# Search for the 256th value: two blocks compared on GpSimd and summed on ScalarE, totals every eleven steps of the products

## The chip, the cores and the metric

One core of one Trainium2 chip runs the whole kernel, in one launch. The metric is the device time in microseconds (us); the kernel before takes 2764.43 us, the median of 3 runs (2760.7 to 2766.13). TensorE (PE in the profile) multiplies, VectorE (DVE), ScalarE (ACT) and GpSimd (POOL) work element by element, and SyncE (SP) issues transfers. Each engine runs its own list of instructions in order, and semaphores are the only link between them: a waiting instruction holds up all that stand behind it on its engine.

## The reference

One step of a small decoder with two branches, a recurrence (RWKV-7) and sparse attention, then a feed-forward part. Two pieces matter here. First, every prompt row attends only to the 256 keys with the highest indexer score:

```python
score = jnp.einsum('bqhs,bqh->bqs', jax.nn.relu(sc), wi.astype(jnp.float32))
score = jnp.where(vis, score, -jnp.inf)
_, idx = lax.top_k(score, n_top)          # n_top = 256 for the 1040 prompt rows
```

Second, the same hidden rows (1040 prompt and 64 sample rows, 1024 wide) are multiplied by the projection `w_in`; its columns for the recurrence and the gates are what the "products" below compute, and the recurrence's columns are mixed with the row before:

```python
h = rms_norm(x, lp['norm1_g']) @ lp['w_in']
prev = jnp.concatenate([shift_prev[:, None, :].astype(p_r.dtype), p_r[:, :-1]], axis=1)
pm = p_r + (prev - p_r) * lp['rwkv_mu']
```

## The kernel before

The function `prompt_and_project` does the prompt's attention and, among it, those products. The prompt's rows lie in nine blocks of up to 128 rows, with 1040, 1024, 896, 768, 640, 512, 384, 256 and 128 visible keys. The seven blocks with more than 256 keys (`SEL`) need the 256th highest score of each row.

**The search.** `bisect` (L926) finds that score bit by bit, in 33 rounds: 1 for the sign, 31 for the bits, 1 to count what is above the result. In a round VectorE compares all scores of a row with a trial value and sums the ones (`tally`, L913; the 1040-key block has only 16 rows and is packed into 128 partitions at L914, the six others are L919). The packed block's partial sums have to be added over partitions: `total` (L520, its matmul is L522) does that on TensorE. VectorE copies the total (L923) and makes the next trial value with three tiny instructions (L938, L940, L943). A round can't begin before the one before is counted. Where each total stands among TensorE's products is written out by a counter (`tick`, L610): one every SPACING = 12 steps, a step being one of the eight 128-deep parts of a plain product.

**The products.** Meanwhile TensorE multiplies the projection. For nine pairs of weight tiles and three column blocks of 368 rows each, so 27 blocks, a block's 2 by 2 arrangement of half-size products is done with seven products in place of eight (`seven`, L468, its matmuls are L480). Product number p (0 to 6) of block m takes 1.25 us and goes to one of four PSUM banks, FA, FB, FD, FE. ScalarE takes each out of its bank (`keep`, L689, its instruction is L691). GpSimd adds the seven to four results: f16 (L857), f167 (L864), then `finish` (L820, three additions L823 to L825). ScalarE then spreads the results to their tiles (`both`, L693, through `evacuate`, L657; L678 and L680 are two of its instructions). A bank can be written again only when it was taken: product 6 needs product 2's bank, product 3 product 0's. ScalarE takes the first product of a block only after f167 of the block before (`f_mid`), and runs `both` of the block before between its products 1 and 2, so product 2 is taken only after `finish`.

GpSimd also makes the mixed weights (`weights_a`, `_b`, `_c`: L807 to L817, four additions of 128x512) for each new pair of tiles, starting in the last column block of the pair before, and the mixing with the row before for two tiles (`mix_tile`, L833 and L834), in the first column block of the next pair. The mixed tile is sent to DRAM by SyncE, and the second column block's `both` of the seventh and earlier tile pairs waits until the transfer from its buffer has landed (`pm_out`, L668). Blocks 12, 13 and 14, used below, are the last column of pair 4 and the first two of pair 5.

**After the products.** The buffer of the products is used again by the choice of the keys: `choose` (L949) may start on VectorE only when the 60th copy is done (L1031). It needs the search's result too. TensorE has six plain products (`unit`, L463) and the scores of the first attention head (L542) still to do, then waits for VectorE's first maximum (`peak_of`, L997), which stands behind three blocks of `choose`.

## Time and profile before

| what | us |
|---|---|
| time, median of 3 runs | 2764.43 |
| the profiled execution's own time | 2757.44 |
| its span, first to last instruction | 2755.6 |
| PE busy | 2571.3 (93%) |
| DVE busy | 1761.6 (64%) |
| ACT busy | 849.2 (31%) |
| POOL busy | 531.9 (19%) |
| products with the search beside them | 318.46 to 577.66 |
| from there to TensorE's next wait for VectorE's end | 577.66 to 608.95 |

The profiled execution is one run, 7.0 us below the median of the timed ones. The shares are means over a span of many stages with different limits: the change lies in a stretch of some 300 us of it.

### The profile page before, as it was taken

The page shows a single profiled execution, that of the slowest core. Times are in us where ns is not written, and L with a number is a line of the kernel's source. Part 1 is how long each engine was busy: PE and PEld are TensorE (multiplying, and loading weights), DVE is VectorE, ACT ScalarE, POOL GpSimd, SP SyncE. Part 2 cuts the span into 40 slices and gives each one's busy share as a digit, 9 for nine tenths or more (in the row PEclk, how much of TensorE's full clock was granted, in tenths as well). Part 3 has the DMA queues.
Part 4 walks back from the last instruction along what each step waited for, and adds up shares of the span by engine and source line. Part 5 has one row for each costly group of instructions (what it writes and reads, how often), then busy time and mean ns, then how long its engine had stood idle before and what let it go on. Part 6 is the DMA issues. An engine that isn't in the chain of part 4 may idle for free.

```text
span 2755.6 us, 51292 instructions
## 1 busy us (share of the span) xinstructions
PE 2571.3 (93%) x19984; PEld 1862.5 (68%) x19984; DVE 1761.6 (64%) x3313; ACT 849.2 (31%) x1914; POOL 531.9 (19%) x757
## 2 busy tenths in 40 slices
PE   8997999989997997889899999998997999999997
PEld 5553699966654323878757997565654665579997
DVE  3556888875444458676679999988732322357666
ACT  2223444325444653111112552012324421122212
POOL 0002366520000000000002662001343451011111
PEclk9998999999998986999999999999998999999999
DMA  8882012231113450000245663343355563533332
GB/s 297 308 291 79 33 64 96 66 110 37 36 52 117 162 165 16 4 27 12 96 134 181 245 241 129 122 141 119 110 170 151 190 200 108 183 130 123 123 123 71
DMA packets 95969, 348.91 MB, mean 127 GB/s; under 512 B 19560, under 2 KB 43976, under 8 KB 74032
## 3 DMA queue, kind: packets, MB, share of 16 engines
q1 hardware_dynamic: 83696, 294.50, 31.2%
q0 software_dynamic: 12032, 51.14, 5.8%
q8 instruction: 159, 2.61, 0.4%
q14 instruction: 82, 0.67, 0.1%
HBM read 289.57 MB, written 55.23 MB: 125 GB/s over the span
## 4 chain that ended last, share of the span: by engine, by line
PE 47%; DVE 7%; DVEq 3%; issue 1%; another core or an unknown queue 1%; DMA 1%; ACT 0%; POOL 0%; ACTq 0%; SPq 0%; POOLq 0%
PE banks L2553 6%; PE banks L2466 5%; PE tl_P L2553 4%; PE banks L2498 4%; PE banks L2484 3%; PE tl_P L2498 3%; PE tl_P L2466 3%; PE banks L2398 3%; PE rc_P L1580 2%; DVE arena L3092 2%; DVE tl_v L3086 2%; DVEq L3090 2%; PE tl_P L2484 2%; PE tl_P L2398 1%; PE banks L1592 1%
## 5 line engine op out<-in xcount | busy, mean ns | idle before, releaser
L162 PE MATMUL pa_PG<-pa_W,base 128*128 128x402 f32 (+1 forms) x576 | 198.5, 504 | 7.8 <-DMA pa_W<-in_w_dsa 7.7
L463 PE MATMUL dp_PS<-base,dp_W 128*128 128x368 f32 x576 | 190.0, 476 | 1.0 <-ACT dp_room_for L723 1.0
L919 DVE TENSOR_SCALAR_CACHE_REDUCE dp_EQ<-dp_SCORE,dp_trial 128x1024 f32<-128x1024 f32 (+1 forms) x186 | 176.0, 946 | 19.5 <-issue 0.5
L2466 PE MATMUL banks<-base,tl_WU 128*128 128x368 f32 x496 | 161.3, 480 | 10.1 <-issue 9.3
L162 PEld LDWEIGHTS pa_PG<-pa_W,base 128*128 128x128 f32 (+1 forms) x576 | 106.7, 187 | 94.5 <-issue 14.2
L2484 PE MATMUL banks<-base,tl_WD 128*128 128x368 f32 x484 | 154.3, 474 | 0.0
L463 PEld LDWEIGHTS dp_PS<-base,dp_W 128*128 128x128 f32 x576 | 104.7, 190 | 64.6 <-issue 8.8
L3036 POOL DMA_INDIRECT arena<-in_cache_kv,tl_PHT x128 | 121.7, 951 | 132.5 <-PE tl_P L2632 96.4
L3086 DVE MAX8 tl_v<-arena 128x8 f32<-128x4100 f32 x32 | 141.8, 4431 | 2.6 <-issue 0.7
L2466 PEld LDWEIGHTS banks<-base,tl_WU 128*128 128x128 f32 x496 | 94.9, 193 | 70.0 <-issue 14.5
L3089 DVE FIND_INDEX8 tl_i<-tl_v,arena 128x8 uint32<-128x4100 f32 x32 | 141.5, 4423 | 0.0
L3092 DVE MATCH_REPLACE8 arena<-tl_v,arena 128x4100 f32<-128x4100 f32 x32 | 141.2, 4414 | 0.0
L2484 PEld LDWEIGHTS banks<-base,tl_WD 128*128 128x128 f32 x484 | 90.5, 190 | 57.1 <-issue 3.7
L480 PE MATMUL dp_PS<-dp_room_for 128*128 128x184 f32 x648 | 111.7, 321 | 0.0
L2738 ACT ACTIVATE arena<-base 128x368 f32<-128x368 f32 x44 | 22.1, 509 | 273.4 <-DVEq L3129 143.4
L480 PEld LDWEIGHTS dp_PS<-dp_room_for 128*128 128x128 f32 x648 | 102.4, 190 | 0.0
L691 ACT ACTIVATE dp_room_for<-dp_PS 128x184 f32<-128x184 f32 x189 | 57.5, 324 | 126.5 <-PE dp_PS L480 120.7
L2705 POOL TENSOR_TENSOR base<-tl_T 128x368 f32<-128x368 f32 x36 | 30.4, 844 | 303.2 <-ACTq L2788 302.3
L2498 PE MATMUL banks<-arena 128*128 128x184 f32 x504 | 85.6, 319 | 1.4 <-DVE arena L3260 1.4
L997 DVE CUSTOM_DVE_ANT_0 dp_room_for<-dp_PS,dp_SCORE 128x1024 f32<-128x1024 f32 (+7 forms) x64 | 48.5, 758 | 57.7 <-PE dp_PS L551 50.3
L2410 PE MATMUL banks<-base,arena 128*128 128x368 f32 x256 | 81.4, 473 | 1.9 <-DMA arena<-in_wo 1.5
L2498 PEld LDWEIGHTS banks<-arena 128*128 128x128 f32 x504 | 80.0, 190 | 1.6 <-issue 1.6
(554 smaller groups left out, 5718.0 us busy)
## 6 DMA issues: line engine op xcount, KB each, us to landing
tl_WU<-in_wu SPq DMA_DIRECT2D x58, 1024.0 KB, 4.9
pa_WQ<-in_wu SPq DMA_DIRECT2D x22, 1024.0 KB, 8.3
wsum<-pa_WS SPq DMA_DIRECT2D x22, 1024.0 KB, 4.9
tl_WD<-in_wd SPq DMA_DIRECT2D x32, 704.0 KB
arena<-wsum SPq DMA_DIRECT2D x21, 1024.0 KB, 7.1
dp_W<-in_w_rw SPq DMA_DIRECT2D x15, 1024.0 KB, 6.5
arena<-in_wb SPq DMA_DIRECT2D x24, 512.0 KB, 3.8
arena<-in_wo SPq DMA_DIRECT2D x24, 512.0 KB, 3.7
```

Source lines behind the costliest of these rows:

```text
L162: last = pe.matmul(PG[0:n, c, 0:NC4], xT[:, k, r:r + n], W[:, c, k, :], start=k == 0, stop=k == KD - 1)
L463: last = pe.matmul(bank(f)[:, 0:w], W[:, t // 2 % 2, k, 128 * (t % 2):128 * (t % 2) + 128], xT[:, k, c:c + w], start=k == 0, stop=k == KD - 1)
L480: last = pe.matmul(out, weights(e, k), moving(k), start=first and k == 0, stop=k == 3, skip_group_check=True)
L919: dve.tensor_scalar(EQ[0:n, 0:m], scored_of(j), values(n, x), None, op, ALU.add, accum_out=result[0:n, x:x + 1])
L2466: last = pe.matmul(out[:, 0:W], WU[:, i % 2, o:o + 128], XN[:, k, :], start=k == 0, stop=k == KD - 1)
L2484: last = pe.matmul(out[:, 0:W], WD[:, i % 3, 128 * e:128 * e + 128], HT[:, f, :], start=f == 0, stop=f == NF - 1)
L2498: last = pe.matmul(out[:, 0:H], weights[:, k, :], moving(k), start=first and k == 0, stop=k == 3, skip_group_check=True)
L2553: last = pe.matmul(out[:, 0:H], weights[:, k, :], moving(k), start=first and k == 0, stop=k == kk - 1, skip_group_check=True)
L3036: pool.indirect_dma_start(out=KV[:, n % 16, t, :], out_offset=None, in_=I["cache_kv"], in_offset=bass.IndirectOffsetOnAxis(ap=PHT[:, 64 * ...
L3086: dve.max(v8[:, :], SC)
L3089: dve.max_index(i8[:, :], v8[:, :], SC)
L3092: dve.match_replace(SC, v8[:, :], SC, TAKEN)
```

## The change

- In each round the comparisons of the two smallest searched blocks (512 and 384 keys) leave VectorE. GpSimd writes their ones and zeros (`compare`) into a buffer that is free then, and ScalarE squares them in place with the sum as accumulator output (`count_in`).
- Three semaphores link the round: VectorE raises `trial_set` when a trial value is there, GpSimd `compared`, ScalarE `counted`, and VectorE waits for `counted` before it ends its round.
- The totals stand every 11 steps, written out ahead as `spots` (block m, product p). At a spot TensorE does the total, ScalarE sums the same round's comparison right after it took that product, and GpSimd makes the next round's comparison in the same block: ahead of f167 for spots at products 0 to 4 (behind `weights_a` or the first `mix_tile`), at the block's end for 5 and 6.
- Three more of them stand ahead of block 1: `compare(0)` in front of the first weights, `compare(1)` in front of `mix_rows(2)`, `count_in(0)` behind plain product 4.
- The spots of blocks 8 to 20 are, as block:product, 8:3, 9:1, 10:0, 10:5, 11:4, 12:2, 13:1, 13:6, 14:5, 15:3, 16:2, 17:0, 17:6, 18:4, 19:3, 20:1; the first are 1:2, 2:1, 2:6, 3:5, 4:3, 5:2, 6:0, 6:6, 7:4, and the last is 25:5.

```diff
-    ROUNDS, SPACING = 33, 12
+    ROUNDS, SPACING = 33, 11
...
+        EASED = (NS - 2, NS - 1)
+        HELD = [T["QIT"][:, a, :] for a in range(2)]
+        spots, spent = {}, KD * (6 - AMONG)
+        for m in range(1, NBL + 1):
+            for p in range(7):
+                spent += 2
+                if spent >= SPACING * (len(spots) + 2) and len(spots) + 1 < ROUNDS:
+                    spots[m, p] = len(spots) + 1
+        assert len(spots) == ROUNDS - 1 and SPACING <= KD * (6 - AMONG) < 2 * SPACING
...
-                        tick(2)
+                        if (m, p) in spots:
+                            total(spots[m, p])
...
-                spent = [0, 0]
-
-                def tick(n):
-                    spent[0] += n
-                    if spent[0] >= SPACING * (spent[1] + 1) and spent[1] < ROUNDS:
-                        total(spent[1])
-                        spent[1] += 1
-
                 for f in range(AMONG, 6):
                     for k in range(KD):
                         unit(f, k, k + 1)
-                        tick(1)
+                        if KD * (f - AMONG) + k + 1 == SPACING:
+                            total(0)
...
-                    for k in range(KD):
-                        unit(f, k, k + 1)
-                        tick(1)
-                for r in range(spent[1], ROUNDS):
-                    total(r)
+                    unit(f)
...
+                def count_in(r):
+                    act.wait_ge(compared, r + 1)
+                    into = over if r == ROUNDS - 1 else count
+                    for a, x in enumerate(EASED):
+                        n, cmp = QB[SEL[x]][1], HELD[a][0:QB[SEL[x]][1], 0:QB[SEL[x]][2]]
+                        act.activation(cmp, cmp, ACT.Square, accum_out=into[0:n, x:x + 1])
+                    act.drain().then_inc(counted, 1)
+
+                def spot(m, p):
+                    if (m, p) in spots:
+                        count_in(spots[m, p])
+
...
                     keep(f1, FA, fa_made, fa_taken, 2 * m - 1)
+                    spot(m, 0)
                     keep(f6, FB, fb_made, fb_taken, 2 * m - 1)
+                    spot(m, 1)
                     if m > 1:
                         both(m - 1)
                     keep(STG[:, 1, H:2 * H], FD, fd_made, fd_taken, 2 * m - 1)
+                    spot(m, 2)
                     keep(STG[:, 0, 0:H], FA, fa_made, fa_taken, 2 * m)
+                    spot(m, 3)
...
                     evacuate(f)
+                    if f == AMONG:
+                        count_in(0)
                 for m in range(1, NBL + 1):
...
+                def compare(r):
+                    pool.wait_ge(trial_set, r + 1)
+                    against, op = (bits, ALU.is_gt) if r == ROUNDS - 1 else (trial, ALU.is_ge)
+                    for a, x in enumerate(EASED):
+                        i, n, m = QB[SEL[x]]
+                        score = SCORE[0:n, first_col[SEL[x]]:first_col[SEL[x]] + m]
+                        least = against[0:n, x:x + 1].bitcast(F32) if r else 0.0
+                        pool.tensor_scalar(HELD[a][0:n, 0:m], score, least, None, op)
+                    pool.drain().then_inc(compared, 1)
+
+                def next_round(m, first, last):
+                    for p in range(first, last):
+                        r = spots.get((m, p), ROUNDS)
+                        if r + 1 < ROUNDS:
+                            compare(r + 1)
...
                 pool.wait_ge(weighted, len(all_pieces))
+                pool.wait_ge(indexed, 1)
+                compare(0)
                 weights_a(PAIRS[0])
                 weights_b(PAIRS[0])
                 weights_c(PAIRS[0])
                 mix_tile(1)
+                compare(1)
                 mix_rows(2)
...
                     if j == 2 and q + 1 in PAIRS:
                         pool.wait_ge(fd_made, 2 * m - 1)
                         weights_a(q + 1)
+                    next_round(m, 0, 5)
                     pool.wait_ge(fb_taken, 2 * m)
                     pool.tensor_tensor(f167, f1, f7, ALU.add)
                     pool.drain().then_inc(f_mid, 1)
@@ -867,6 +907,7 @@
...
+                    next_round(m, 5, 7)
                 finish(NBL)
...
-                        if x:
+                        if x and x not in EASED:
                             dve.tensor_scalar(EQ[0:n, 0:m], scored_of(j), values(n, x), None, op, ALU.add,
                                               accum_out=result[0:n, x:x + 1])
                             dve.drain()
+                    dve.wait_ge(counted, r + 1)
                     dve.wait_ge(totalled, r + 1)
...
-                        dve.drain()
                         if b:
+                            dve.drain()
                             dve.tensor_scalar(trial[:, :], bits[:, :], 1 << (b - 1), None, ALU.bitwise_xor)
-                            dve.drain()
+                        dve.drain().then_inc(trial_set, 1)
                     tally(32, lambda n, x: bits[0:n, x:x + 1].bitcast(F32), ALU.is_gt, over)
```

How GpSimd's instructions stand in block 12 and the start of block 13, before (L807 and L809 are `weights_a`, L864 f167, L813 `weights_b`, L823 to L825 `finish`):

```order
L807 TENSOR_TENSOR dp_room_for<-dp_W 128x512 [waits dp_w_in1,dp_fd_made]
L809 TENSOR_TENSOR dp_room_for<-dp_room_for,dp_W 128x512
L864 TENSOR_TENSOR dp_room_for<-dp_room_for 128x184 [waits dp_fb_taken]
L813 TENSOR_TENSOR dp_room_for<-dp_W 128x512
L823 TENSOR_TENSOR dp_room_for<-dp_room_for 128x184 [waits dp_fe_taken,dp_fd_taken]
L824 TENSOR_TENSOR dp_room_for<-dp_room_for 128x184
L825 TENSOR_TENSOR dp_room_for<-dp_room_for 128x184
```

and now (L827, L829 `weights_a`, L855 the comparison, L904 f167, L833 `weights_b`, L843 to L845 `finish`):

```order
L827 TENSOR_TENSOR dp_room_for<-dp_W 128x512 [waits dp_w_in1,dp_fd_made]
L829 TENSOR_TENSOR dp_room_for<-dp_room_for,dp_W 128x512
L855 TENSOR_SCALAR base<-dp_SCORE,dp_trial 128x512 [waits dp_trial_set]
L855 TENSOR_SCALAR base<-dp_SCORE,dp_trial 128x384
L904 TENSOR_TENSOR dp_room_for<-dp_room_for 128x184 [waits dp_fb_taken]
L833 TENSOR_TENSOR dp_room_for<-dp_W 128x512
L843 TENSOR_TENSOR dp_room_for<-dp_room_for 128x184 [waits dp_fe_taken,dp_fd_taken]
L844 TENSOR_TENSOR dp_room_for<-dp_room_for 128x184
L845 TENSOR_TENSOR dp_room_for<-dp_room_for 128x184
```

Two instructions with a wait for a new trial value now stand between `weights_a` and f167.

GpSimd in block 13, from f16 on, before (L857 f16, L833 and L834 `mix_tile`, L864 f167):

```order
L857 TENSOR_TENSOR dp_room_for<-dp_room_for 128x184 [waits dp_fb_taken,dp_fa_taken]
L833 TENSOR_TENSOR dp_PMT<-dp_PMT,dp_PX 128x1040 [waits pa_summed]
L834 TENSOR_TENSOR dp_PMT<-dp_PMT,dp_PX 128x64
L864 TENSOR_TENSOR dp_room_for<-dp_room_for 128x184 [waits dp_fb_taken]
L833 TENSOR_TENSOR dp_PMT<-dp_PMT,dp_PX 128x1040 [waits pa_summed]
L834 TENSOR_TENSOR dp_PMT<-dp_PMT,dp_PX 128x64
L823 TENSOR_TENSOR dp_room_for<-dp_room_for 128x184 [waits dp_fe_taken,dp_fd_taken]
```

and now (L896 f16, L869 and L870 `mix_tile`, L904 f167):

```order
L896 TENSOR_TENSOR dp_room_for<-dp_room_for 128x184 [waits dp_fb_taken,dp_fa_taken]
L869 TENSOR_TENSOR dp_PMT<-dp_PMT,dp_PX 128x1040 [waits pa_summed]
L870 TENSOR_TENSOR dp_PMT<-dp_PMT,dp_PX 128x64
L855 TENSOR_SCALAR base<-dp_SCORE,dp_trial 128x512 [waits dp_trial_set]
L855 TENSOR_SCALAR base<-dp_SCORE,dp_trial 128x384
L904 TENSOR_TENSOR dp_room_for<-dp_room_for 128x184 [waits dp_fb_taken]
L869 TENSOR_TENSOR dp_PMT<-dp_PMT,dp_PX 128x1040 [waits pa_summed]
L870 TENSOR_TENSOR dp_PMT<-dp_PMT,dp_PX 128x64
L855 TENSOR_SCALAR base<-dp_SCORE,dp_trial 128x512 [waits dp_trial_set]
L855 TENSOR_SCALAR base<-dp_SCORE,dp_trial 128x384
L843 TENSOR_TENSOR dp_room_for<-dp_room_for 128x184 [waits dp_fe_taken,dp_fd_taken]
```

One comparison stands between the first `mix_tile` and f167, another between the second and `finish`.

ScalarE in block 12, from `both` of block 11 on, before (L678 and L680 are `both`, L691 are the takings of products 2 to 6):

```order
L678 ACTIVATE dp_PMT<-dp_room_for,dp_rest 128x368 [waits dp_f_done]
L680 ACTIVATE dp_PX<-dp_room_for,dp_mu 128x368
L678 ACTIVATE dp_PMT<-dp_room_for,dp_rest 128x368 [waits dp_f_done]
L680 ACTIVATE dp_PX<-dp_room_for,dp_mu 128x368
L691 ACTIVATE dp_room_for<-dp_PS 128x184 [waits dp_fd_made]
L691 ACTIVATE dp_room_for<-dp_PS 128x184 [waits dp_fa_made]
L691 ACTIVATE dp_room_for<-dp_PS 128x184 [waits dp_fb_made]
L691 ACTIVATE dp_room_for<-dp_PS 128x184 [waits dp_fe_made]
L691 ACTIVATE dp_room_for<-dp_PS 128x184 [waits dp_fd_made]
```

and now (L677 and L679 `both`, L690 the takings, L703 the sums of ones):

```order
L677 ACTIVATE dp_PMT<-dp_room_for,dp_rest 128x368 [waits dp_f_done]
L679 ACTIVATE dp_PX<-dp_room_for,dp_mu 128x368
L677 ACTIVATE dp_PMT<-dp_room_for,dp_rest 128x368 [waits dp_f_done]
L679 ACTIVATE dp_PX<-dp_room_for,dp_mu 128x368
L690 ACTIVATE dp_room_for<-dp_PS 128x184 [waits dp_fd_made]
L703 ACTIVATE base,dp_count<-base 128x512 [waits dp_compared]
L703 ACTIVATE base,dp_count<-base 128x384
L690 ACTIVATE dp_room_for<-dp_PS 128x184 [waits dp_fa_made]
L690 ACTIVATE dp_room_for<-dp_PS 128x184 [waits dp_fb_made]
L690 ACTIVATE dp_room_for<-dp_PS 128x184 [waits dp_fe_made]
L690 ACTIVATE dp_room_for<-dp_PS 128x184 [waits dp_fd_made]
```

The sums, with a wait for GpSimd's comparison, now stand between the takings of products 2 and 3.

## Rows read from the trace of the kernel before

**Rows 1.** Product stage: start:end, length, busy time per engine, clock, DMA.

```profile
318.46:577.66 259.20, 249.52 (x1575) 244.17 (x1574) 226.32 (x566) 113.32 (x329) 153.29 (x194) 0.99 0.22 75
```

**Rows 2.** TensorE's waits, 315 to 590 us: total, times, longest.

```profile
PE dp_PS L480 <- ACT dp_room_for L691: 5.3, 5, 2.1
PE dp_PS L522 <- DVEq L915: 4.0, 9, 0.8
```

**Rows 3.** Timeline of TensorE: start, duration, line, idle time before.

```profile
424.07 1.49 PE L480 MATMUL dp_PS<-base,dp_room_for 128*128 128x184 f32 x8 [0.82 <-ACT dp_room_for L691]
...
452.39 1.49 PE L480 MATMUL dp_PS<-base,dp_room_for 128*128 128x184 f32 x8
```

**Rows 4.** Timeline of GpSimd over the same stretch.

```profile
424.43 0.57 POOL L864 TENSOR_TENSOR dp_room_for<-dp_room_for 128x184 f32<-128x184 f32 x1 [4.63 <-ACT dp_room_for L691]
425.99 0.57 POOL L823 TENSOR_TENSOR dp_room_for<-dp_room_for 128x184 f32<-128x184 f32 x1 [0.99 <-ACT dp_room_for L691]
...
428.55 0.57 POOL L857 TENSOR_TENSOR dp_room_for<-dp_room_for 128x184 f32<-128x184 f32 x1 [0.93 <-ACT dp_room_for L691]
429.38 1.27 POOL L807 TENSOR_TENSOR dp_room_for<-dp_W 128x512 f32<-128x512 f32 x1 [0.25 <-PE dp_PS L480]
...
432.24 0.57 POOL L864 TENSOR_TENSOR dp_room_for<-dp_room_for 128x184 f32<-128x184 f32 x1 [0.18 <-ACT dp_room_for L691]
...
439.02 2.40 POOL L833 TENSOR_TENSOR dp_PMT<-dp_PMT,dp_PX 128x1040 f32<-128x1040 f32 x1 [0.18 <-ACTq L687]
...
442.62 2.03 POOL L833 TENSOR_TENSOR dp_PMT<-dp_PMT,dp_PX 128x1040 f32<-128x1040 f32 x1 [0.18 <-issue]
444.60 0.31 POOL L834 TENSOR_TENSOR dp_PMT<-dp_PMT,dp_PX 128x64 f32<-128x64 f32 x1
```

**Rows 5.** Timeline of ScalarE over the same stretch.

```profile
423.60 0.97 ACT L691 ACTIVATE dp_room_for<-dp_PS 128x184 f32<-128x184 f32 x4
...
437.44 0.60 ACT L678 ACTIVATE dp_PMT<-dp_room_for,dp_rest 128x368 f32<-128x368 f32 x1
...
440.60 0.54 ACT L691 ACTIVATE dp_room_for<-dp_PS 128x184 f32<-128x184 f32 x2
...
450.53 0.31 ACT L670 ACTIVATE dp_PX<-dp_sh,dp_mu 128x8 f32<-128x8 f32 x1 [2.37 <-DMA PM_dram<-dp_PMT]
```

**Rows 6.** Timeline of VectorE: end of a search round, next start.

```profile
419.48 0.75 DVE L919 TENSOR_SCALAR_CACHE_REDUCE dp_EQ<-dp_SCORE,dp_trial 128x512 f32<-128x512 f32 x1
...
421.03 0.16 DVE L923 COPY dp_count<-dp_PS 128x1 f32<-128x1 f32 x1
...
422.02 0.35 DVE L914 TENSOR_SCALAR_CACHE_REDUCE dp_EQ<-dp_PACK,dp_trial 128x130 f32<-128x130 f32 x1
```

**Rows 7.** Groups of VectorE, search for the 256th value.

```profile
L943 DVE TENSOR_SCALAR dp_trial<-dp_bits 128x7 int32<-128x7 int32 x30 | 11.5, 384 | 2.6 <-issue 0.4
```

**Rows 8.** Groups by form: nearest relatives of the added instructions.

```profile
L728 ACT ACTIVATION_READ_ACCUMULATOR dp_room_for<-dp_room_for,dp_npeak 128x1 f32 x65 | 12.1, 186 | 0.0
L728 ACT ACTIVATE dp_room_for<-dp_room_for,dp_npeak 128x512 f32<-128x512 f32 x8 | 5.8, 722 | 0.8
L728 ACT ACTIVATE dp_room_for<-dp_room_for,dp_npeak 128x384 f32<-128x384 f32 x8 | 4.9, 615 | 0.8
L1833 ACT ACTIVATE rc_SQ<-base 128x512 f32<-128x512 f32 x8 | 5.0, 631 | 18.5 <-DVEq L1945 18.5
L1567 POOL MEMSET rc_XP<- 128x1280 f32 x1 | 1.2, 1164 | 0.2 <-issue 0.2
```

**Rows 9.** Timeline after the products: ScalarE, VectorE, TensorE.

```profile
579.99 1.12 ACT L676 ACTIVATE dp_PX<-dp_room_for 128x368 f32<-128x368 f32 x2 [1.80 <-POOLq L826]
...
585.69 0.93 DVE L1032 MEMSET dp_room_for<- 128x1040 f32 x1 [0.32 <-issue]
...
608.95 3.72 PE L551 MATMUL dp_PS<-base,QT 64*128 64x512 f32 x8 [12.28 <-DVEq L1002]
```

**Rows 10.** A stretch of halved clock, columns as in Rows 1.

```profile
366.60:370.00 3.40, 3.40 (x14) 3.40 (x13) 3.11 (x8) 0.47 (x2) 1.56 (x3) 0.52 0.00 0
```

More of the change, by code:

```diff
@@ L344, in prompt_and_project @@
          same_in, tallied, totalled, xf_made, wf_made, fa_made, fa_taken, fb_made, fb_taken, fd_made, fd_taken, fe_made,
-         fe_taken, f_mid, f_done) = (nc.alloc_semaphore(name=f"dp_{n}") for n in names)
+         fe_taken, f_mid, f_done, trial_set, compared, counted) = (nc.alloc_semaphore(name=f"dp_{n}") for n in names)
         w_in, gate_out, pm_out, spilled = (
@@ L466, in unit, with seven @@
                         last.then_inc(product, 1)
-                def seven(m, tick):
+                def seven(m):
                     q, j = BLOCKS[m - 1]
@@ L476, in seven, with multiply @@
                     mix = lambda i: lambda k: XF[:, j, i, k, :]
-                    def multiply(out, weights, e, moving, first, made):
+                    def multiply(p, out, weights, e, moving, first, made):
                         for k in range(4):
@@ L487, in seven @@
                     pe.wait_ge(fa_taken, 2 * m - 2)
-                    multiply(FA, raw, 0, left, True, fa_made)
+                    multiply(0, FA, raw, 0, left, True, fa_made)
                     pe.wait_ge(xf_made, j + 1)
@@ L934, in bisect @@
                     dve.tensor_scalar(trial[:, :], bits[:, :], 1 << 30, None, ALU.bitwise_xor)
-                    dve.drain()
+                    dve.drain().then_inc(trial_set, 1)
                     for b in range(30, -1, -1):
```

22 lines of the change are left out of this document (12 added, 10 removed).

## The prediction

> **What bounds the kernel now.** I read the page's chain first: it follows TensorE through most of the span, so I took the stretch of the change by itself. In the product stage TensorE is busy 249.5 of 259.2 us, at a clock of 0.99 [rows 1]. So little can be won inside it: TensorE's labelled waits are 5.3 us for ScalarE's taking of a product and 4.0 us for VectorE's part of a total [rows 2]. Then I asked who is late in those 5.3 us, and for that the timelines of the four engines over one period have to be laid side by side. From product 6 of block 11 (424.07) to product 6 of block 14 (452.39) are 28.32 us [rows 3], for 21 products. In that period GpSimd, only 59% busy over the stage (153 of 259 us, [rows 1]), has hardly an idle moment from `weights_a` at 429.38 to the end of the second `mix_tile` at 444.91 [rows 4]. From there the tile goes to DRAM, ScalarE waits for it until 450.53 [rows 5], does `both` and the takings, and TensorE's product 6 starts at 452.39, 7.48 us behind `mix_tile`'s end. GpSimd's `weights_a` in its turn starts on product 2 of the block before, 5.31 us behind product 6 of the last period. That is a ring: whatever is added to GpSimd between f167 and the second `mix_tile` lengthens every period of 28 us. In block 11 itself f167 has 4.63 us of idle time ahead of it [rows 4]; that is the only large gap.
>
> After the stage VectorE is late: ScalarE has the 60th copy done at 581.1 (579.99 + 1.12), but VectorE is in the last round of the search until 585.69, and TensorE idles 12.28 us for what follows from it [rows 9].
>
> **The parts.** *Taken from VectorE:* two comparisons and sums a round, 419.48 to 421.03, so 1.55 us [rows 6]. The end of the round, from the copy of the total to the next round's first comparison, stays: 0.99 us [rows 6], more on average, since the third tiny instruction has a mean of 0.38 us [rows 7] and others sometimes grow alike. With semaphores I take 1.3 us from ScalarE's sum to the next trial value on GpSimd (bounds 1.0 and 1.5). VectorE's round is then shorter than 5.5 products, and its lag, 4.0 us of TensorE's waits, is gone.
>
> *Count on ScalarE:* a square of 128x512 is 0.63 us, an exponential with sum 0.72 and for 384 keys 0.62, the accumulator's reading 0.19 each [rows 8]. By the squares 0.63 + 0.5 + 0.37 = 1.5, by the exponentials 1.7. I take 1.55 (bounds 1.35, 1.7), since the instruction is the square. It stands ahead of the takings of the next products.
>
> *Comparison on GpSimd:* the trace has no one-input comparison there. From below: a fill of 1280 elements takes 1.16 us, 0.91 ns an element [rows 8], so 0.8 us for 896. From above: a two-input addition of 512 takes 1.27 us [rows 4], so some 2.2 us for both. A comparison has one input, so I stay near the fill, and with two starts and the drain take 1.3 us (bounds 0.8, 2.2).
>
> The Trainium skill, GPSIMD Engine Reference, section 4.1, says that GpSimd is about half VectorE's speed with two inputs but near line rate with one. By its section 3.1, 1.03 cycles of 1.2 GHz an element, 896 elements are 0.77 us, an estimate from that page without the starts; by the comparison price of that estimate the sum below would end about 9 us lower. No row here shows it.
>
> *One period walked through*, t counted from 424.07, spots 11:4, 12:2, 13:1, 13:6. ScalarE has taken product 4 of block 11 at 0.3 [rows 5]; count to 1.85; trial value 3.15; comparison to 4.45; f167 to 5.1 (before: 424.43 + 0.57, so 0.9); `finish`, three additions of 0.57 and a drain, to 7.0; `both` of block 11 and the taking of product 2 to 9.8; count of spot 12:2 to 11.35; trial value 12.65. GpSimd has meanwhile done `weights_a` (2.86 us, 429.38 to 432.24) by 10.75 and waits; comparison to 13.95; f167 14.65; `weights_b` 16.1; `finish` 17.95; ScalarE's `both` (437.44 to 440.60, 3.16 us, [rows 5]) 21.15; first `mix_tile` (start to f167 and on, 439.02 to 442.62, holds 2.85 and 0.75) to 24.1; comparison, whose trial value is long there, to 25.4; f167 26.15; second `mix_tile` to 28.45, where the trace before has 444.91 - 424.07 = 20.84. With the same 7.48 us behind it product 6 of block 14 starts at 35.9 in place of 28.3: **+7.6 us a period**. In words: three comparisons 3.9, two counts 3.1, two trial values 2.6, less 2.0 absorbed.
>
> *The other periods*, walked the same way with their own spots: blocks 2 to 5 and 5 to 8 (four spots each, among them product 6, where the comparison stands ahead of `finish`) +7 each; 8 to 11 (8:3, 9:1, 10:0; two trial values are ready when GpSimd comes) +5; 14 to 17 +7; 17 to 20, whose tiles have no wait for a transfer, +5. With 7.6 that is 38.6. The start, with two comparisons ahead of the first mixed rows and two counts among the first takings, another +5. From block 21 there is no `mix_tile`, GpSimd has room, and VectorE's waits go: -2. **Stage: +42** (38.6 + 5 - 2).
>
> *The end:* the search is done blocks earlier, so `choose` starts on the copy: 585.69 - 581.1 = 4.6, with 0.2 us of semaphore -4.4. TensorE waits there, so all of it counts: late next is still VectorE's choosing. Totals: the same 33, no cost.
>
> Sum: 2757.4 (the profiled execution's own time) + 42 - 4.4 = 2795. The median of the runs shown lies 7.0 us above that execution, so the forecast for a median is **2802 us**.
>
> Over a stretch the low bounds (comparison -0.5 three times, count -0.2 and trial -0.3 twice) take off 2.5 us, the high ones (+0.9, +0.15, +0.2) add 3.4. Over six periods and the start: -17 and +22. The forecast's own range is 2785 to 2824.
>
> **Rivals.** *1. The work falls into idle time* (the other side: faster). For it: GpSimd idles 41% of the stage and ScalarE 56% [rows 1], and the 4.63 us ahead of f167 would hold three comparisons. Against it: the spots stand where they stand in the list, not in the gap, and each is chained to a count and a trial value. It decides if the second `mix_tile` ends less than about 1 us later than before in a period. Then only VectorE's gains are left: -4.0 in the stage and -4.4 at the end, and some unlabelled time around the totals, 2764 - 12 = 2752.
>
> *2. Half absorbed.* VectorE's waits had already loosened the ring in the periods where they fell, and if the gaps of 4.6 us take up one comparison, count and trial value in each period (4.1 us), the stage costs 42 - 6 x 4.1 = 17, and the time is 2764 + 17 - 4 = 2777. The walk says that only 2.0 are absorbed.
>
> *3. More than the sum.* TensorE's 2.1 us wait was followed by 3.4 us at a clock of 0.52 [rows 2, 10], 1.2 GHz instead of 2.4. The new waits at product 6 are 4 to 7 us long. Each such stretch costs 1.7 us if nothing hides it; in the walk `weights_a` starts 2.6 us behind its product, which hides it, but not at every place. Six times 1.7 is +10: 2812. VectorE's tiny instructions could also grow: the mean of L943 against its neighbours shows it [rows 7].
>
> The Trainium skill, SBUF - State Buffer, "Who interferes with whom", says that a `tensor_scalar` without accumulator on VectorE can take the port pair it shares with GpSimd, and that whichever comes second is fully blocked. The 0.38 us mean agrees. It speaks against the change, since GpSimd gets a third more work; a whole tail at its upper bound in each round would add 0.2 us twice a period, about 2 us.
>
> **Chances.** Forecast 0.70, rival 1 0.10, rival 2 0.12, rival 3 0.08. The smallest difference that a measurement of this kernel can tell is about 0.2%, 5.5 us. Faster by more: 0.10. Within: 0.03, the low end of rival 2. Slower: 0.87. The range for 8 in 10 is 2770 to 2826: it leaves out rival 1 and what lies below the half-absorbed case or beyond the high bounds.
>
> **What would show it.** TensorE's product stage of 259.2 us near 301, by waits at product 6 (L489 in the new kernel) for ScalarE. Product 6 to product 6 over blocks 11 to 14 near 36 us. ScalarE idle ahead of L703 for a comparison, GpSimd idle ahead of L855 for a trial value, in place of the gap ahead of f167. VectorE waits for the count in nearly every round. The memset ahead of `choose` within 0.3 us of the last copy, and TensorE's wait after the products near 8 us instead of 12.28. A stage near 250 us would prove me wrong, and so would comparisons of over 2.2 or under 0.8 us.

## The result and the profile after

| what | us |
|---|---|
| time after, median of 4 runs (2823.34 to 2826.35) | 2825.05 |
| time before in the same job, median of 4 runs | 2763.91 |
| ratio, 95% interval | 1.0216 [1.0201, 1.0230] |
| the profiled execution's own time, its span | 2825.28, 2823.4 |

The kernel is slower by 61 us; 2802 were forecast. The product stage, shown by the same view as [rows 1] (start and end, length, busy time of PE, PEld, DVE, ACT and POOL, granted clock, DMA share, GB/s):

```profile
318.46:644.50 326.04, 271.28 (x1581) 264.01 (x1580) 182.57 (x443) 145.37 (x458) 243.50 (x262) 0.92 0.17 60
```

It is 326.0 us long where it was 259.2. GpSimd went from 153 to 243.5 us of work, three quarters of the longer stage. The waits of the changed kernel from 300 to 680 us (engine, tile and line, what it waited for: total, times, longest), against [rows 2]:

```profile
DVE dp_count L965 <- ACTq L704: 94.5, 29, 7.1
PE dp_PS L489 <- ACT dp_room_for L690: 54.6, 27, 6.0
ACT dp_room_for L690 <- POOLq L905: 52.7, 14, 9.5
ACT dp_PMT L677 <- POOLq L846: 46.8, 16, 6.2
POOL base L855 <- DVEq L986: 40.9, 22, 4.8
...
ACT base L703 <- POOLq L856: 15.2, 6, 3.7
```

Read from the second row on, it is one chain. TensorE waits for ScalarE's takings of its products: 5.3 us in 5 waits before, 54.6 in 27 now. ScalarE waits for what stands behind GpSimd's f167 (L905) and behind its `finish` (L846), and GpSimd waits for VectorE's trial values (L986), which in turn wait for ScalarE's sums (L704). VectorE's 94.5 us are idle time: by themselves they cost nothing, but each ends with a sum that a trial value needs. TensorE's waits for VectorE's part of a total are gone.

The two added instructions and their groups by form (count, then busy time and mean ns of one, then the idle time before them), where [rows 8] held only relatives:

```profile
L855 POOL TENSOR_SCALAR base<-dp_SCORE,dp_trial 128x512 f32<-128x512 f32 x31 | 48.4, 1561 | 42.3 <-DVEq L986 40.5 <-issue 1.7
L855 POOL TENSOR_SCALAR base<-dp_SCORE,dp_trial 128x384 f32<-128x384 f32 x31 | 38.5, 1241 | 0.0
...
L703 ACT ACTIVATE base<-base 128x512 f32<-128x512 f32 x32 | 20.2, 631 | 15.2 <-POOLq L856 15.2
L703 ACT ACTIVATE base<-base 128x384 f32<-128x384 f32 x32 | 16.6, 519 | 0.0
L703 ACT ACTIVATION_READ_ACCUMULATOR base<-base 128x1 f32 x64 | 12.7, 198 | 0.0
```

A round's comparison on GpSimd is 1.56 + 1.24 us. The timeline of GpSimd in the new period from block 11 to block 14 (start, duration, line; x2 joins both blocks' comparisons), against [rows 4]:

```profile
459.45 2.78 POOL L855 TENSOR_SCALAR base<-dp_SCORE,dp_trial 128x512 f32<-128x512 f32 x2 [4.85 <-DVEq L986]
462.41 0.57 POOL L904 TENSOR_TENSOR dp_room_for<-dp_room_for 128x184 f32<-128x184 f32 x1 [0.18 <-issue]
...
469.84 2.78 POOL L855 TENSOR_SCALAR base<-dp_SCORE,dp_trial 128x512 f32<-128x512 f32 x2 [1.52 <-DVEq L986]
472.80 0.57 POOL L904 TENSOR_TENSOR dp_room_for<-dp_room_for 128x184 f32<-128x184 f32 x1 [0.18 <-issue]
...
481.78 2.78 POOL L855 TENSOR_SCALAR base<-dp_SCORE,dp_trial 128x512 f32<-128x512 f32 x2 [0.20 <-issue]
484.74 0.57 POOL L904 TENSOR_TENSOR dp_room_for<-dp_room_for 128x184 f32<-128x184 f32 x1 [0.18 <-issue]
```

From the start of a comparison to the start of f167 (L904) are 2.96 us: 462.41 - 459.45, 472.80 - 469.84, 484.74 - 481.78. Ahead of the first, GpSimd stood idle for 4.85 us. What ended that is on the timelines of ScalarE and VectorE:

```profile
457.13 0.64 ACT L703 ACTIVATE base<-base 128x512 f32<-128x512 f32 x1
...
458.47 0.32 ACT L690 ACTIVATE dp_room_for<-dp_PS 128x184 f32<-128x184 f32 x1
```

```profile
458.42 0.16 DVE L965 COPY dp_count<-dp_PS 128x1 f32<-128x1 f32 x1 [4.13 <-ACTq L704]
...
459.15 0.17 DVE L985 TENSOR_SCALAR dp_trial<-dp_bits 128x7 int32<-128x7 int32 x1
```

The two sums take 1.33 us with the drain (457.13 to about 458.47), the trial value is out 1.0 us later, and the comparison starts. So each round hands over three times on this path: ScalarE to VectorE, VectorE to GpSimd, and GpSimd back to ScalarE. TensorE's product 6 in blocks 11 and 14, the places of [rows 3]:

```profile
456.98 2.79 PE L489 MATMUL dp_PS<-base,dp_room_for 128*128 128x184 f32 x8 [4.20 <-ACT dp_room_for L690]
...
496.31 2.79 PE L489 MATMUL dp_PS<-base,dp_room_for 128*128 128x184 f32 x8 [5.79 <-ACT dp_room_for L690]
```

The period is 39.33 us instead of 28.32. Both rows show 2.79 us for eight matmuls that took 1.49 before: behind such a wait TensorE runs at the lower of its two clocks (granted 0.50 from 456.98 to 459.77), and the stage's mean granted clock is 0.92 instead of 0.99. After the stage, against [rows 9]:

```profile
645.45 1.12 ACT L675 ACTIVATE dp_PX<-dp_room_for 128x368 f32<-128x368 f32 x2 [1.79 <-POOLq L846]
```

```profile
646.88 0.93 DVE L1074 MEMSET dp_room_for<- 128x1040 f32 x1 [21.97 <-ACTq L686]
```

```profile
670.49 3.58 PE L561 MATMUL dp_PS<-base,QT 64*128 64x512 f32 x8 [8.56 <-DVEq L1044]
```

The memset starts 0.3 us behind the last copy, and TensorE's wait shrinks from 12.28 to 8.56 us.

Over the stage, from the start of product 6 (the times are those of TensorE's timeline, as above):

| stretch | before | after | more | forecast |
|---|---|---|---|---|
| up to block 2 | 336.20 | 343.96 | +7.8 | +5 |
| blocks 2 to 5 | 30.05 | 36.57 | +6.5 | +7 |
| 5 to 8 | 29.80 | 38.93 | +9.1 | +7 |
| 8 to 11 | 28.02 | 37.52 | +9.5 | +5 |
| 11 to 14 | 28.32 | 39.33 | +11.0 | +7.6 |
| 14 to 17 | 28.81 | 36.23 | +7.4 | +7 |
| 17 to 20 | 29.26 | 36.78 | +7.5 | +5 |
| 20 to 27 | 65.96 | 72.57 | +6.6 | -2 |
| TensorE's wait after | 12.28 | 8.56 | -3.7 | -4.4 |

The sum is +61.8, the distance of the medians 61.1. (The profiled execution of before was a quick one; the two profiles are 67.8 us apart, and the 6 us more lie behind this part of the kernel, where nothing was changed.)

### The profile page after: what moved, and what is told of

It is laid out like the page before. It is cut to its first block, busy times and chain, and to the rows that moved or that the text cites. A ratio compares the mean times of both kernels' runs of the same rounds, so it can differ in the third digit from the quotient of the medians.

```text
span 2823.4 us, 51391 instructions
## 1 busy us (share of the span) xinstructions
PE 2595.4 (92%) x19984; PEld 1885.7 (67%) x19984; DVE 1711.1 (61%) x3181; ACT 882.0 (31%) x2046; POOL 622.9 (22%) x823
## 4 chain that ended last, share of the span: by engine, by line
PE 45%; DVE 7%; DVEq 3%; issue 1%; another core or an unknown queue 1%; DMA 1%; ACT 0%; POOL 0%; ACTq 0%; POOLq 0%; SPq 0%
PE banks L2595 6%; PE banks L2508 5%; PE tl_P L2595 4%; PE banks L2540 4%; PE banks L2526 3%; PE tl_P L2540 3%; PE rc_P L1622 2%; PE banks L2440 2%; PE tl_P L2508 2%; DVE arena L3134 2%; DVE tl_v L3128 2%; DVEq L3132 2%; PE tl_P L2526 1%; PE banks L1634 1%; PE tl_P L2440 1%
## 5 line engine op out<-in xcount | busy, mean ns | idle before, releaser
L472 PEld LDWEIGHTS dp_PS<-base,dp_W 128*128 128x128 f32 x576 | 104.7, 190 | 64.8 <-issue 8.8
L960 DVE TENSOR_SCALAR_CACHE_REDUCE dp_EQ<-dp_SCORE,dp_trial 128x1024 f32<-128x1024 f32 (+1 forms) x124 | 133.8, 1079 | 14.3 <-issue 1.0
L489 PE MATMUL dp_PS<-base,dp_W 128*128 128x184 f32 x432 | 87.6, 351 | 11.8 <-ACT dp_room_for L690 11.8
L855 POOL TENSOR_SCALAR base<-dp_SCORE,dp_trial 128x512 f32<-128x512 f32 (+1 forms) x62 | 86.1, 1401 | 42.3 <-DVEq L986 40.5
L489 PE MATMUL dp_PS<-base,dp_room_for 128*128 128x184 f32 x216 | 49.2, 381 | 42.5 <-ACT dp_room_for L690 42.5
L489 PEld LDWEIGHTS dp_PS<-base,dp_W 128*128 128x128 f32 x432 | 78.5, 213 | 14.6 <-ACT dp_room_for L690 14.2
```

The lines of the kernel that those rows point to most:

```text
L472: last = pe.matmul(bank(f)[:, 0:w], W[:, t // 2 % 2, k, 128 * (t % 2):128 * (t % 2) + 128], xT[:, k, c:c + w], start=k == 0, stop=k == KD - 1)
L489: last = pe.matmul(out, weights(e, k), moving(k), start=first and k == 0, stop=k == 3, skip_group_check=True)
L960: dve.tensor_scalar(EQ[0:n, 0:m], scored_of(j), values(n, x), None, op, ALU.add, accum_out=result[0:n, x:x + 1])
```

## The experiments

Theory: GpSimd is the tight link of a ring, so its comparisons count in full, three to a period of three blocks, and the sums that the trial values wait for come on top. (Three is the count of the period that the prediction walked, whose fourth comparison stands behind the second `mix_tile`. In the changed kernel's trace 23 comparisons start between product 6 of block 2 and that of block 20, not 18.) Rivals: the sums on ScalarE, the spacing of eleven, or the mere load of GpSimd wherever it stands. Ratios are to the kernel before on the same chip in the same job, whose medians were 2760.55, 2765.62 and 2740.69 us in the three timed jobs (a ratio on record can differ from the quotient of the medians by about 0.1%); "blocks 2 to 27" is the time from product 6 of the one to that of the other, 240.2 us before and 297.9 after.

**Spacing alone.** The kernel before, totals every eleven steps.

```
-    ROUNDS, SPACING = 33, 12
+    ROUNDS, SPACING = 33, 11
```

> The kernel before with totals every 11 steps and nothing else. Theory (the loss is GpSimd's comparisons, ScalarE's sums and the hand-overs inside the ring): spacing alone does not touch the ring, but VectorE's rounds still take 8.2 us, so the last total, now 31 steps ahead of the products' end, is held by VectorE until about 578 us and 19 us of products stand behind it: products end near 597 instead of 577.7, and the wait behind them shrinks by 4; about 2779 us, with TensorE's waits at the totals up by some 20 us. Rival (the denser totals are what cost the 61 us): near 2825. Rival (spacing is free): 2764.

2780.95 us, 1.0069 [1.0045, 1.0093]. VectorE's long round doesn't fit in eleven steps. TensorE's waits:

```profile
PE dp_PS L522 <- DVEq L915: 23.9, 20, 3.3
PE dp_PS L551 <- DVEq L1002: 8.3, 1, 8.3
```

Waits for VectorE's part of a total grow from 4.0 to 23.9 us, and 4.0 come back at the end.

**The change at spacing twelve.**

```
-    ROUNDS, SPACING = 33, 11
+    ROUNDS, SPACING = 33, 12
-                if spent >= SPACING * (len(spots) + 2) and ...
+                if spent >= min(SPACING * (len(spots) + 2), KD * (6 - AMONG) + 14 * NBL) and ...
```

> The changed kernel with totals every 12 steps, spots written out in the same way (the last one behind the last product). Theory: 3.5 rounds instead of 3.8 in a period of three column blocks, each worth about 5 us in the ring (comparison 2.96, sum 1.5, next trial 1.3, less what is absorbed): about 2813 us. Rival (the spacing of 11 is the cause): the loss goes, 2765 or less.

2818.27 us, 1.0216 [1.0199, 1.0233]: the ratio of the change itself. The closer totals are not what makes it slow.

**Half the comparison.** GpSimd compares only half of each block's columns; the other half is left out of the computation, and ScalarE still sums the full width.

```
+                        m = m // 2                      # in compare
-  act.activation(cmp, cmp, ACT.Square, accum_out=...)
+  act.activation(cmp, cmp, ACT.Copy, scale=2.0, accum_out=...)
```

> The changed kernel in which GpSimd compares only the first half of the columns of its two blocks (the other half is left out and filled with zeros once), while ScalarE still sums the full width, so only the comparison's duration is changed, from 2.78 to about 1.5 us. Theory: three comparisons a period in the ring, six periods and the start: 20 times 1.3 is 26, about 2799 us. Rival (GpSimd's duration is covered, and the waiting chain of sums and trial values is what counts): within 5 us of 2825.

2792.96 us, 1.0108 [1.0084, 1.0133]; blocks 2 to 27 take 268.9 us. The halves took:

```profile
L856 POOL TENSOR_SCALAR base<-dp_SCORE,dp_trial 128x256 f32<-128x256 f32 x31 | 28.5, 921 | 43.4 <-DVEq L990 42.6 <-issue 0.8
L856 POOL TENSOR_SCALAR base<-dp_SCORE,dp_trial 128x192 f32<-128x192 f32 x31 | 23.6, 760 | 0.0
```

That is 1.12 us less a round (1561 + 1241 - 921 - 760 ns). From block 2 to block 20 the kernel gained 22.3 us (203.1 instead of 225.4). That is as much as 20 comparisons at 1.12 us: 18, three a period, would give 20.2, and all 23 of them 25.8. So GpSimd's time counts nearly in full. Two reservations: the profile is that of the longest of four runs (2783.06 to 2797.29 us), and TensorE's products 0, 3 and 6 took 11.3 us less busy time there, at a higher clock, some of which may be in the gain.

**The comparison later in the block.**

```
-                    next_round(m, 0, 5)
...
-                    next_round(m, 5, 7)
+                    next_round(m, 0, 7)
```

> The changed kernel with every comparison at the end of its block, behind f167 (and behind the second mix_tile where there is one). Same work, other place. Theory: of the three comparisons in the ring the one between the two mix_tiles leaves it, 3 us in each of six periods, and f167 is no longer held: about 2805 us. Rival (GpSimd's sheer load, 75% busy in the stage, sets the pace): no change, 2825.

2828.97 us, 1.0252 [1.0235, 1.0269]: missed, nothing was won. The waits of this kernel show why:

```profile
ACT base L703 <- POOLq L856: 49.3, 16, 7.0
...
POOL base L855 <- DVEq L985: 23.6, 15, 2.7
```

GpSimd waits 17 us less for trial values (40.9 before the edit), but ScalarE now waits 49.3 us instead of 15.2 for comparisons, and the takings of the products stand behind that wait. The stall moved from one link of the ring to the next. That the load alone sets the pace, the rival with the right number, doesn't follow: the next kernel has the same load on GpSimd and is faster.

**Without ScalarE's sums.** VectorE waits for the comparison itself. The counts of the two blocks are left out of the computation; a small copy puts neighbours' counts in their place.

```
-                    spot(m, 0)        # and spots 1 to 6, and count_in(0)
-                    dve.wait_ge(counted, r + 1)
+                    dve.wait_ge(compared, r + 1)
```

> The changed kernel without ScalarE's two sums of a round: GpSimd still makes both comparisons in every round, and VectorE waits for them itself; the two eased blocks' counts are copied from neighbouring columns (one small copy more on VectorE), so that the counts of those blocks are left out of the computation. My theory (GpSimd's comparisons set the pace of the three-block ring, ScalarE's sums add what lies between a comparison and VectorE's totals and what precedes the takings): a sum of 1.33 us start to end lies in some 15 to 17 rounds on the path, about 19 us in all, so about 2806 us. Rival A (the sums are the cost, GpSimd has room): most of the 64 us goes, under 2780 us. Rival B (GpSimd's load alone sets the pace): within 5 us of 2825.

2800.67 us, 1.0141 [1.0120, 1.0162]; blocks 2 to 27 take 274.6 us. Both rivals fall. From block 2 to 20 the gain is 17.7 us, 2.9 a period, about two sums of 1.33. The sums may be worth a little more, since VectorE's three small instructions took 1.39 us a round here instead of 0.90.

**Without GpSimd's comparisons.** ScalarE sums as much, out of zeroed tiles into a spare column; the comparisons of the two blocks are left out of the computation.

```
-                    act.wait_ge(compared, r + 1)
+                    act.wait_ge(compared, 1)
+                    act.wait_ge(trial_set, r + 1)
...
-                    next_round(m, 0, 5)
-                    next_round(m, 5, 7)
```

> The changed kernel without GpSimd's comparisons: ScalarE still sums 512 and 384 columns twice over in every round, from zeroed tiles into a spare column, as soon as the trial is set; the two blocks' counts are copied from neighbours, so that their comparison is left out of the computation. Spacing 11. My theory: the comparison costs 2.96 us in each of three places of each period of three blocks, so without it the stage of both kinds of work falls back near 260 to 268 us and the kernel to about 2762 us (the changed kernel's end is 3.7 us shorter than before, and totals at every eleventh step alone were +20 us with VectorE's long count, which here is short). Rival A (the sums are the cost): at least 2800 us. Rival B (spacing 11 is what costs): 2780 us or more.

2753.20 us, 0.9961 [0.9949, 0.9973], 9 us under what I expected; blocks 2 to 27 take 232.8 us, less than before the change. This is the run that decides: sums, the exchange with VectorE and spacing eleven together cost no more than VectorE's shorter round gives back, as long as GpSimd has no part. With 170.1 us from block 2 to 20, the whole comparison adds 55.3 and half of it 33.0; 18 times 2.96 is 53.3, and 18 times 1.84 (2.96 - 1.12) is 33.1. That these agree doesn't make the 55.3 us the comparison's alone. With its sums the changed kernel takes 225.4 us, without them 207.7, and with the sums alone 170.1: the comparisons are worth 55.3 us where the sums stand too, and the kernel with comparisons and no sums is only 37.6 us above this one. The sums, which show no cost here, add 2.9 us a period where GpSimd also compares. A kernel with neither wasn't run, so the two can't be priced apart.

**Sign and sum in one instruction of ScalarE, two blocks.** GpSimd is out of it.

```
- act.activation(cmp, cmp, ACT.Square, accum_out=into[0:n, x:x + 1])
+ act.activation(HELD[a][0:n, 0:m], SCORE[0:n, first_col[SEL[x]]:first_col[SEL[x]] + m], ACT.Sign,
+                bias=trial[0:n, x:x + 1].bitcast(F32), scale=-1.0, accum_out=count[0:n, x:x + 1])
...
+                            half = QB[SEL[x]][2] / 2 + 0.5
+                            dve.tensor_scalar(result[:, x:x + 1], result[:, x:x + 1], -0.5, half, ALU.mult, ALU.add)
```

The sum of the signs of trial minus score is the number of scores below the trial value less the number above it; halved, turned round and with half the width it is the number above. The 0.5 on top makes one score that equals the trial value count fully, and changes nothing against the threshold of 256 when there is none. Two scores that both equal the trial value count 1.5 instead of 2, so the form isn't exact for such rows. The first and the last round stay on VectorE whole.

> Totals at every eleventh step as in the changed kernel, but ScalarE makes the comparison and its sum in one instruction for each of the two blocks (the sign of trial minus score, with its accumulator, turned into a count on VectorE by one small operation a column); GpSimd has no part in the search. The first and the last round stay on VectorE whole. My theory: GpSimd's ring is as before the change, ScalarE has the same two sums as in the changed kernel (1.33 us a round), VectorE's round is short; the time is that of the kernel without comparisons, about 2762 us, within 6 us. Rival (the exchange between VectorE and ScalarE or the spacing is what costs, whoever compares): 2785 us or more.

2752.52 us, 0.9964 [0.9950, 0.9977]: the time of the kernel without comparisons (2753.20), as the theory had it, but 3.5 us under the stated range; the rival falls. ScalarE's row for this:

```profile
444.84 0.72 ACT L704 ACTIVATE base<-dp_SCORE,dp_trial 128x512 f32<-128x512 f32 x1
445.45 0.19 ACT L704 ACTIVATION_READ_ACCUMULATOR base<-dp_SCORE,dp_trial 128x1 f32 x1
445.55 0.60 ACT L704 ACTIVATE base<-dp_SCORE,dp_trial 128x384 f32<-128x384 f32 x1
```

Comparison and sum together cost ScalarE 0.72 us for 512 columns; the sum alone was 0.63. GpSimd's 1.56 us bought 0.09.

**The same for one block, spacing twelve.** The edit is that of the kernel above, with

```
-        EASED = (NS - 2, NS - 1)
+        EASED = (NS - 1,)
```

> As the kernel with the sign on ScalarE, but for the last block of 384 columns alone and with totals at every twelfth step, as in the kernel before. VectorE's round is 0.5 us shorter than before, ScalarE has 0.75 us more a round. My theory: the ring of GpSimd is untouched, the round's time is off the path but for the takings right behind a sum: 2757 us, between 2752 and 2764, the same as or just under the kernel before. Rival (every instruction put on ScalarE lands on the path through its takings): 33 sums of 0.75 us, 2780 us or more.

2751.84 us, 0.9961 [0.9946, 0.9975]: 0.2 us under the range, and the rival falls.

**The same for two blocks at spacings ten and twelve.** The edits are the kernel with two blocks above and SPACING = 10, then 12.

> The kernel with comparison and sum in one instruction of ScalarE for two blocks, with totals at every tenth step. With eleven it took 2752.5 us, and its TensorE still waits 8.2 us for the weights of the selection at the end. If the round of VectorE (comparisons, sum, small operations) fits in ten steps of the products, the search ends some 3 steps for each ten rounds earlier and the end wait falls by up to 8 us: 2745 to 2750. Rival (ten steps are shorter than a round, as eleven were with VectorE's long count): TensorE waits at the totals, 2760 or more.

0.9992 [0.9979, 1.0005] (2739.38 us on a chip where the kernel before takes 2740.69): the gain is gone, as the rival had it. TensorE waits at the totals again, and the end gives nothing more back:

```profile
PE dp_PS L532 <- DVEq L937: 14.5, 17, 1.9
PE dp_PS L561 <- DVEq L1030: 8.2, 1, 8.2
```

> The same kernel with totals at every twelfth step, as in the kernel before. It tells what the spacing is worth where nothing waits for GpSimd: if it is worth only the wait at the end, this takes 2752.5 plus about 3.4 us (11.6 instead of 8.2 at the end, as in the kernel with one block at twelve steps), 2756; if the closer totals cost something in the products, it is at or under 2752.

2724.27 us against 2740.69, 0.9948 [0.9932, 0.9964]: the lowest ratio of all, though its interval overlaps those of the kernels with one block and with spacing eleven. My expectation for the end was wrong: the wait for the choosing's weights is 8.1 us, not 11.6. At twelve steps with two blocks off VectorE the search is just done when the last copy is, so spacing eleven had nothing more to win: VectorE waits 0.3 us for the last copy ahead of its memset. And it costs something: TensorE's waits for VectorE's part of a total are 0.2 us at twelve steps, 3.2 at eleven and 14.5 at ten.

**What a comparison costs GpSimd by itself.** Two kernels with timed instructions on 128x512 elements and a drain behind each: first behind the products, then earlier, ahead of the last `finish` but one, where VectorE is idle. Each ran once, and only the durations are used.

> The changed kernel, and behind GpSimd's last products of the blocks six instructions of GpSimd on 128x512 elements with a drain behind each, where it is otherwise idle: comparison with a constant, comparison with a value per partition, addition of a constant, subtraction of a value per partition, copy, and addition of two tensors. In the changed kernel the comparison with a value per partition took 1.56 us and GpSimd's addition of two tensors 1.27. My theory (the price is that of the one-input scalar form itself): all of the first four between 1.4 and 1.6 us here too, with nothing beside them, the copy under 1, the addition near 1.1 to 1.3. Rival (the price came from VectorE and the others working beside it in the stage): comparison at 0.8 to 1.1 us here.

> The same instructions of GpSimd on 128x512 elements, the addition of a constant twice, but two blocks earlier, where the search is over and VectorE is idle for some 20 us. In the first probe the addition of a constant took 3.06 us with VectorE working beside it, and the comparison with a value per partition 1.87. My theory (the one-input scalar form costs about 1.5 us by itself, and what was above it was VectorE's work beside it): all four scalar forms between 1.45 and 1.6 us here, the addition of a constant too, the copy near 0.6, the addition of two tensors near 1.27. Rival (an addition of a constant is slow by itself, and its comparison partner's 1.56 in the stage was inflated by VectorE): addition of a constant near 3 us both times, and the comparison with a value per partition under 1.3.

The first, in GpSimd's timeline (comparison with a constant, with a value per partition, addition of a constant, subtraction of a value per partition, copy, addition of two tensors):

```profile
646.14 1.49 POOL L915 TENSOR_SCALAR base<-base 128x512 f32<-128x512 f32 x1 [0.20 <-issue]
647.80 1.87 POOL L917 TENSOR_SCALAR base<-base,dp_bits 128x512 f32<-128x512 f32 x1 [0.17 <-issue]
649.83 3.06 POOL L919 TENSOR_SCALAR base<-base 128x512 f32<-128x512 f32 x1 [0.16 <-issue]
653.05 1.57 POOL L921 TENSOR_SCALAR base<-base,dp_bits 128x512 f32<-128x512 f32 x1 [0.16 <-issue]
654.76 0.61 POOL L923 COPY base<-base 128x512 f32<-128x512 f32 x1
655.52 1.30 POOL L925 TENSOR_TENSOR base<-base 128x512 f32<-128x512 f32 x1
```

The second, with the addition of a constant twice, and the stretch's windows row (VectorE's busy time is the 0.00):

```profile
634.40 1.49 POOL L862 TENSOR_SCALAR base<-base 128x512 f32<-128x512 f32 x1 [0.20 <-issue]
636.06 1.56 POOL L863 TENSOR_SCALAR base<-base,dp_bits 128x512 f32<-128x512 f32 x1 [0.17 <-issue]
637.79 1.50 POOL L864 TENSOR_SCALAR base<-base 128x512 f32<-128x512 f32 x1 [0.16 <-issue]
639.45 1.49 POOL L865 TENSOR_SCALAR base<-base 128x512 f32<-128x512 f32 x1 [0.16 <-issue]
641.11 1.57 POOL L866 TENSOR_SCALAR base<-base,dp_bits 128x512 f32<-128x512 f32 x1 [0.17 <-issue]
642.82 0.61 POOL L867 COPY base<-base 128x512 f32<-128x512 f32 x1
643.58 1.04 POOL L868 TENSOR_TENSOR base<-base 128x512 f32<-128x512 f32 x1
```

```profile
634.00:645.00 11.00, 9.16 (x59) 8.88 (x57) 0.00 (x0) 1.30 (x4) 9.64 (x9) 1.00 0.00 0
```

With VectorE idle, all scalar forms take 1.49 to 1.57 us, so the comparison's 1.56 us in the stage are its own price and not contention. The addition of a constant that took 3.06 us beside VectorE's operations takes 1.50 alone, and the comparison that took 1.87 takes 1.56. In the first probe these two lay outside my 1.4 to 1.6 us.

## Why the prediction was right, and which step was off

The direction and the place were right: TensorE waits at product 6 for ScalarE, ScalarE for GpSimd, GpSimd for a trial value, VectorE for counts in 29 rounds; the waits for totals are gone; the memset follows the last copy. The number was 23 us low: 1 us above the forecast's own range (2785 to 2824), and 1 us inside the range for 8 in 10 (2770 to 2826). That it fell inside is luck more than sizing. Of the steps these were off:

1. **The comparison's price.** The step "I stay near the fill, and with two starts and the drain take 1.3 us (bounds 0.8, 2.2)" failed: it is 2.96 us, above even the bound, as the forecast's own condition said would prove it wrong. The fill, at 0.91 ns an element, was no guide for a comparison at 2.5; at 2.96 - 1.3 = 1.66 us more, three a period, six periods give 29.9 us. The inference "a comparison has one input" from the fill, and the Trainium skill's statement (GPSIMD Engine Reference, section 4.1) that one-input operations run near line rate, went the same way; the measurement decides against both for this form: 1.56 us for 512 elements, slower than the 1.27 us of a two-input addition, while the copy's 0.61 us comes nearer to that page.

2. **What is absorbed.** With the right prices (comparison +1.66 three times, sum -0.22 twice) the six periods would have come to 38.6 + 29.9 - 2.6 = 65.9 us. Measured are 51.1, so 14.8 us more were absorbed, 2.5 a period beyond the 2.0 of the walk. The period that was walked, 11 to 14, has hardly a part in that: 7.6 + 5.0 - 0.4 would be 12.1, and it grew by 11.0. The rest lies in the other five, of which the prediction gives only results. The kernel without comparisons shows that sums and trial values have room in the ring when GpSimd doesn't compare; which of them were absorbed in the changed kernel stays open. With 2.5 us a period the truth lies between the forecast's none and the 4.1 of the rival of the half absorbed work, nearer the rival. The two errors partly hid each other, and that is luck: without the second the forecast would have been some 15 us further off.

3. **The last blocks.** "GpSimd has room: -2" failed: +6.6 us. Without the mixing of a tile GpSimd does have room, but it still stands idle ahead of a comparison for its trial value (1.99 us at 592.56, 3.16 at 601.94); the kernel without comparisons takes 62.6 us there, so 9.9 of the 72.57 come with the comparisons.

4. **Start and end.** +7.8 instead of +5, from the same price; -3.7 instead of -4.4: the memset came 4.3 us earlier behind the copy, but from it to the multiplication were 23.61 us instead of 23.26, and TensorE's work before it ended 0.2 us earlier behind the copy.

The sum (1.33 us for 1.55) and the trial value's way (1.0 to 1.1 us where no small instruction was long) lay inside their bounds. Rival 3's halved clock is there: the matmuls of products 0 and 3, and of product 6, hold 87.6 and 49.2 us,

```profile
L489 PE MATMUL dp_PS<-base,dp_W 128*128 128x184 f32 x432 | 87.6, 351 | 11.8 <-ACT dp_room_for L690 11.8
L489 PE MATMUL dp_PS<-base,dp_room_for 128*128 128x184 f32 x216 | 49.2, 381 | 42.5 <-ACT dp_room_for L690 42.5
```

against 77.2 + 38.6 in the version with twelve steps and two blocks on ScalarE, which hardly waits: 21 us more of busy time. How much of it lies on the ring stays open. It could have entered where the first addition of `weights_a` waits for product 2, in eight of nine cases, but it didn't: ahead of all nine GpSimd is idle for 0.3 us in total.

```profile
L827 POOL TENSOR_TENSOR dp_room_for<-dp_W 128x512 f32<-128x512 f32 x9 | 11.4, 1272 | 0.3 <-issue 0.2
```

The rule that VectorE's and GpSimd's operations block each other (the Trainium skill, SBUF - State Buffer, "Who interferes with whom") doesn't show on GpSimd's side of the stage: 1.561 us a comparison there, 1.56 with VectorE idle. On VectorE's side the trace agrees with it. The three small instructions of a round (L980, L982, L985) took 0.17 us in all 56 cases in which GpSimd was idle; beside its two-input operations they took up to 1.5, here 0.45 and 0.46:

```profile
475.75 0.45 DVE L982 TENSOR_TENSOR dp_bits<-dp_bits,dp_step 128x7 int32<-128x7 int32 x1
476.13 0.57 POOL L845 TENSOR_TENSOR dp_room_for<-dp_room_for 128x184 f32<-128x184 f32 x1
476.27 0.46 DVE L985 TENSOR_SCALAR dp_trial<-dp_bits 128x7 int32<-128x7 int32 x1
```

On average the three take 0.90 us a round instead of 0.51, so 12 us over the rounds, and before the change it was 0.97. How much of that reaches a trial value that GpSimd waits for isn't shown. Of GpSimd's own rows the 1.87 and 3.06 us of the first probe are the two where it may have acted.

## What to carry to other kernels

Work moved to an engine that is 59% busy can still cost nearly its full length: ask whether that engine's chain closes a ring with the bound engine, and whether the new work stands at fixed places of it. Price an operation from the same form on the same engine; where the trace has none, time it in a spare stretch first, since here the wrong relative was off by more than a factor of two. And look for the version with no handover: one instruction of ScalarE did comparison and sum for 0.09 us more than the sum alone, and turned the loss of 2.2% into a gain of 0.5% [0.4, 0.7].

## What the runs showed of the hardware

- GpSimd, 128x512 elements of 32 bits: comparison, addition or subtraction with a constant or a value per partition 1.49 to 1.57 us, addition of two tensors 1.04 to 1.30, copy 0.61. At this size one input with a scalar was slower than two inputs (in the probes the addition read one tensor twice; in the stage it took 1.27 with two). For the comparison the price is near 2.5 ns an element plus 0.28 us (1561, 1241, 921 and 760 ns for 512, 384, 256 and 192).
- The same addition of a constant took 3.06 us beside VectorE at work and 1.50 beside VectorE idle, the comparison with a value per partition 1.87 and 1.56; each seen once.
- VectorE's instructions on 128x7 elements took 0.17 us in all 90 cases, before and after, in which GpSimd was idle, and between 0.17 and 1.9 us beside a two-input operation of GpSimd.
- ScalarE's sign with a bias per partition and a sum takes 0.72 us for 512 columns, as its exponential with a sum did [rows 8].
